# Attention and expert gathers of a transformer layer in one program block, with the expert queries computed between the rows, and weights in batches of four

## The reference

```python
def peer_block(hb, w_q, sub_keys, u_tab, v_tab):
    q = (hb @ w_q).reshape(n, PEER_HEADS, PEER_QDIM)             # 8 heads, 2 x 128
    s1 = jnp.einsum('nhd,kd->nhk', q1, sub_keys[0])              # 128 scores a half
    s2 = jnp.einsum('nhd,kd->nhk', q2, sub_keys[1])
    v1, i1 = lax.top_k(s1, 16); v2, i2 = lax.top_k(s2, 16)
    top_s, pos = lax.top_k(v1[..., :, None] + v2[..., None, :], 16)
    g = jax.nn.softmax(top_s)
    act = jax.nn.gelu(jnp.einsum('nhkd,nd->nhk', u_tab[expert], hb))
    return jnp.einsum('nhk,nhkd->nd', g * act, v_tab[expert])
```

## Time and profile before

| what | us |
|---|---|
| median of 3 runs | 3617.58 (3615.84 to 3617.71) |
| profiled execution, its own time | 3618.12 |
| its span, first to last instruction | 3616.3 |
| busy: PE, DVE, POOL, ACT | 2665.0, 2239.5, 1350.0, 430.3 |
| first gather of the latents' experts, of the last layer's | 1964.35, 2936.63 |

### The profile page before, as it was taken

One profiled execution on the slowest core, in us unless ns is written; L12 is line 12 of the kernel. 1 busy time (PEld: TensorE's weight loads), 2 busy tenths in 40 slices (PEclk: granted clock), 3 DMA queues, 4 the chain that ended last, 5 costly groups with the idle time before them and its releaser, 6 DMA issues. The chain is left out here.

```text
span 3616.3 us, 24758 instructions
## 1 busy us (share of the span) xinstructions
PE 2665.0 (74%) x7868; PEld 1434.3 (40%) x7868; DVE 2239.5 (62%) x5144; ACT 430.3 (12%) x1222; POOL 1350.0 (37%) x1082
## 2 busy tenths in 40 slices
PE   6788839459958648993575877878866757787777
PEld 1423324437625446741344333333333533333333
DVE  1316655686666686665867777777526157777774
ACT  0200001110000110000110111111112101111111
POOL 0000002365564265664444444545300034545442
PEclk9999869569988759996887898888878878888898
DMA  7154426389988378998776999999850259999996
GB/s 256 70 204 152 152 97 239 119 286 335 389 301 315 119 259 305 392 358 314 238 246 241 421 420 420 420 420 420 348 184 24 88 207 421 421 421 421 421 422 248
DMA packets 258261, 1043.06 MB, mean 288 GB/s; under 512 B 20342, under 2 KB 36838, under 8 KB 192340
## 3 DMA queue, kind: packets, MB, share of 16 engines
q0 software_dynamic: 147456, 805.37, 56.5%
q1 hardware_dynamic: 102928, 220.69, 16.8%
q10 hardware_dynamic: 7748, 15.43, 1.2%
HBM read 1038.69 MB, written 2.72 MB: 288 GB/s over the span
## 5 line engine op out<-in xcount | busy, mean ns | idle before, releaser
L1077 POOL DMA_INDIRECT sb_beside_slots<-in_peer_uv,sb_beside_chosen x512 | 610.8, 1193 | 706.1 <-issue 363.3
L1001 PE MATMUL psum<-sb_last_rows,sb_last_H 128*128 128x512 f32 x768 | 401.4, 687 | 168.7 <-ACT sb_last_H L985 168.7
L1001 PE MATMUL psum<-sb_latents_rows,sb_latents_diag 128*128 128x512 f32 x640 | 351.2, 714 | 165.0 <-ACT sb_latents_diag L985 165.0
L1050 DVE SCALAR_TENSOR_TENSOR sb_beside_slots<-sb_beside_slots,sb_beside_H 128x1024 f32<-128x1024 f32 x256 | 312.3, 1221 | 228.8 <-DMA sb_beside_slots<-in_peer_uv,sb_beside_chosen 227.2
L894 POOL DMA_INDIRECT sb_last_rows<-in_peer_uv,sb_last_scores x192 | 236.7, 1233 | 363.0 <-PE psum L1001 257.2
L1069 DVE SCALAR_TENSOR_TENSOR sb_xc<-sb_beside_slots,sb_beside_small,sb_xc 128x1024 f32<-128x1024 f32 x254 | 325.5, 1282 | 8.0 <-DMA sb_beside_slots<-in_peer_uv,sb_beside_chosen 6.2
L1001 PEld LDWEIGHTS psum<-sb_last_rows,sb_last_H 128*128 128x128 f32 x768 | 166.8, 222 | 402.7 <-issue 203.7
L894 POOL DMA_INDIRECT sb_latents_rows<-in_peer_uv,sb_latents_scores x160 | 203.2, 1270 | 292.8 <-PE psum L1001 247.3
L921 DVE SCALAR_TENSOR_TENSOR sb_last_rows<-sb_last_rows,sb_last_H 128x1024 f32<-128x1024 f32 x192 | 231.3, 1222 | 110.3 <-DMA sb_last_rows<-in_peer_uv,sb_last_scores 110.3
L172 PE MATMUL psum<-sb_f_arena,sb_f_ring 128*128 128x256 f32 (+1 forms) x1344 | 292.9, 381 | 5.4 <-issue 5.4
L1001 PEld LDWEIGHTS psum<-sb_latents_rows,sb_latents_diag 128*128 128x128 f32 x640 | 144.5, 231 | 370.6 <-ACT sb_latents_diag L985 194.2
(11 more groups left out here) (468 smaller groups left out, 3733.9 us busy)
## 6 DMA issues: line engine op xcount, KB each, us to landing
sb_f_ring<-in_w_ff SPq DMA_DIRECT2D x32, 2048.0 KB, 12.8
sb_context_ring<-in_ada_w SPq DMA_DIRECT2D x24, 2048.0 KB, 7.9
sb_f_ring<-in_w_in SPq DMA_DIRECT2D x8, 2048.0 KB, 14.4
sb_f_ring<-in_w_in SPq DMA_DIRECT2D x6, 1904.0 KB, 12.6
sb_context_ring<-in_peer_w_q SPq DMA_DIRECT2D x8, 1024.0 KB, 10.0
sb_beside_slots<-in_peer_uv,sb_beside_chosen POOLq DMA_INDIRECT x512, 6.2
sb_f_ring<-in_w_out SPq DMA_DIRECT2D x4, 2048.0 KB, 7.8
sb_latents_ring<-in_peer_w_q SPq DMA_DIRECT2D x4, 2048.0 KB, 10.8
```

The lines of the kernel that those rows point to most:

```text
L1001: done = e.matmul(st.pair(("acc", g))[:, half, :], diag[:, n % (2 * ROWS), :], v_of(n)[:, half * 512:(half + 1) * 512], start=(f == 0 and ...
L1050: e.scalar_tensor_tensor(out=self.u_slot[s % 4], in0=self.u_slot[s % 4], scalar=1.0, in1=self.H[:, s // (PH * TOPK), :], op0=ALU.mult, op1 ...
L1077: return e.indirect_dma_start(out=to, out_offset=None, in_=self.table, in_offset=bass.IndirectOffsetOnAxis(ap=at, axis=0), element_offset= ...
```

## The change

1. For the latents' and the last layer, `attention` no longer runs a block of its own. It returns its engine programs as a `Front`, and `experts` runs them at the head of its own block. The context's block stays.
2. The 16 query blocks move from the end of `attention` into `experts`. Blocks 0 to 3 stand before the rows; block t + 4 is computed in turn t, its queries ahead of the turn's sums on PE and its scores after half of them. w_q comes in eight loads of 1 MB (256 columns) into the halves of ring slot 2. `SC` holds three heads, not all.
3. The turns are ordered head by head, both tiles of a head in turn, so both accumulators stay open.
4. `weights` takes 4 rows, not 8, and the diagonals have four batches of room. Routing of the turn after next is spread over the four batches.
5. The head loop runs `more(2)`. What is left of `Beside` runs right after the second norm.
6. `layer_memory` lays all buffers out once; slots for rows overlay attention's buffers. There are 14 of them in the latents' layer and 15 in the last.

```diff
-    st.run(sync, scalar, vector, gpsimd, tensor, beside and beside.sems[0])
+    if context:
+        st.run(sync, scalar, vector, gpsimd, tensor)
+    return Front(st, sync, scalar, vector, gpsimd, tensor, lambda e: e.wait_ge(*st.computed(("qkv", 2, h_tiles[-2]))))
...
         for i in range(n_heads + 2):
-            more(1)
+            more(2)
...
+        more(Beside.STEPS)
+        if not context:
+            return
...
+    turns = [(g, f) for f in range(PH) for g in range(NT)]
...
+    wq_half = [sb["ring"][2][:, 2048 * j:2048 * (j + 1)].rearrange("p (k n) -> p k n", k=KT) for j in range(2)]
+    bank_q, bank_sc = [psum[:, 4 + j, 0:S] for j in range(2)], [psum[:, 6 + j, 0:S] for j in range(2)]
...
+    ahead = lambda t: t + 4 if t + 4 < 2 * PH else None
+
+    def sync(e):
+        front.sync(e)
+        front.slot_free(e)
+        for f in range(PH):
+            if f >= 2:
+                e.wait_ge(q_done, 2 * f - 2)
+            e.dma_start(wq_half[f % 2], wq[:, :, f * S:(f + 1) * S]).then_inc(wq_in[f % 2], 16)
+        e.nop()
...
+        keep_scores(0)
+        keep_scores(1)
         for q in (0, 1):
             half_of(q, 0)
             half_of(q, 1)
             route_sums(e, own, rt, top_ready)
             picks(q)
+            keep_scores(2 + q)
         for q in range(len(turns)):
             more = q + 2 < len(turns)
...
+            for j in range(TOPK // BATCH):
+                b = TOPK // BATCH * q + j
+                for r in range(BATCH):
+                    dot(b * BATCH + r)
+                if more and j < 2:
+                    half_of(q + 2, j)
+                if more and j == 2:
+                    route_sums(e, own, rt, top_ready)
+                if more and j == 3:
+                    picks(q + 2)
                 weights(b)
...
+            if ahead(q):
+                keep_scores(ahead(q))
...
+            if b >= 4:
+                e.wait_ge(added, BATCH * (b - 3))
+            for r in range(BATCH):
+                e.activation(diag[:, (b % 4) * BATCH + r, :], C("ident"), ACT.Copy, scale=w[:, r:r + 1]).then_inc(diag_ready, 1)
...
+        queries(0)
+        queries(1)
+        scores(0)
+        queries(2)
+        scores(1)
+        queries(3)
+        scores(2)
+        scores(3)
+        for q in range(len(turns)):
+            if ahead(q):
+                queries(ahead(q))
+            sums(4 * q)
+            sums(4 * q + 1)
+            if ahead(q):
+                scores(ahead(q))
+            sums(4 * q + 2)
+            sums(4 * q + 3)
...
+    slots = [ring[:, j // 2, 2048 * (j % 2):2048 * (j % 2 + 1)] for j in range(4)] + [work[:, 0:2048], work[:, 2048:4096]]
+    slots += [pair(gains, 0), aux[:, 0:2048], pair(mod, 0), *spare]
```

More of the change, by code:

```diff
@@ L271, in attention @@
         plan += wq_plan[7:8]
[L272 to L275, removed]
+    wq_of = lambda b: ("q", b // 2 * 2 + 1)
+    wq_cols = lambda b: (b % 2) * P
     wqkv_of = {g[1]: g for _, g, _ in plan if g[0] == "qkv"}
@@ L987, in scalar @@
+        keep_queries(0)
+        keep_queries(1)
+        keep_queries(2)
         route(0)
+        keep_queries(3)
         route(1)
         for q in range(len(turns)):
-            weights(2 * q)
+            weights(4 * q)
+            if ahead(q):
+                keep_queries(ahead(q))
+            weights(4 * q + 1)
+            weights(4 * q + 2)
             if q + 2 < len(turns):
                 route(q + 2)
-            weights(2 * q + 1)
+            weights(4 * q + 3)
     def tensor(e):
-        for n in range(n_rows):
-            g, f = turns[n // TOPK]
-            k = n % TOPK
-            e.wait_ge(diag_ready, n + 1)
-            for half in range(2):
-                done = e.matmul(st.pair(("acc", g))[:, half, :], diag[:, n % (2 * ROWS), :], v_of(n)[:, half * 512:(half + 1) * 512],
-                                start=(f == 0 and k == 0), stop=(f == PH - 1 and k == TOPK - 1))
-            done.then_inc(added, 1)
@@ L1005, in experts, with queries, scores @@
-    st.run(idle, scalar, vector, gpsimd, tensor)
+        front.tensor(e)
+        def queries(b):
+            f = b // 2
+            e.wait_ge(wq_in[f % 2], 16 * (f // 2 + 1))
+            if b >= 2:
+                e.wait_ge(q_copied, b - 1)
+            matmuls(e, bank_q[b % 2], [(wq_half[f % 2][:, k, (b % 2) * P:(b % 2 + 1) * P], hT[:, k, :]) for k in range(KT)]).then_inc(q_done, 1)
+        def scores(b):
+            e.wait_ge(q_copied, b + 1)
+            if b >= 2:
+                e.wait_ge(sc_copied, b - 1)
+            for j in range(2):
+                done = e.matmul(bank_sc[b % 2][:, j * P:(j + 1) * P], qbuf[b % 2][:, j * P:(j + 1) * P], sub[:, 2 + b % 2, :], start=True, stop=True)
+            done.then_inc(sc_done, 1)
@@ new lines, in sums @@
+        def sums(b):
+            for n in range(b * BATCH, (b + 1) * BATCH):
+                g, f = turns[n // TOPK]
+                k = n % TOPK
+                e.wait_ge(diag_ready, n + 1)
+                for half in range(2):
+                    done = e.matmul(st.pair(("acc", g))[:, half, :], diag[:, n % (4 * BATCH), :], v_of(n)[:, half * 512:(half + 1) * 512],
+                                    start=(f == 0 and k == 0), stop=(f == PH - 1 and k == TOPK - 1))
+                done.then_inc(added, 1)
@@ L1818, in expert_memory @@
[L1818 to L1829 removed]
+    sb["ring"] = [ring[:, j, :] for j in range(3)]
@@ L1830, in expert_memory @@
+    sb["slots"] = slots
     return sb
@@ L1868, in build @@
         st.run(load, idle, idle, idle, idle)
-        def layer(layer, part, held, beside=None):
-            with ExitStack() as inner:
-                attention(nc, sems, psum, attention_memory(mem(inner, f"{part}_"), held, part), A, C, xs, kept, layer, part, beside)
         with ExitStack() as both:
```

202 lines of the change are left out of this document (100 added, 102 removed).

## The result

The kernel after takes 3563.02 us (median of four runs, 3561.24 to 3564.98) against 3617.57 (3615.84 to 3617.71) before: a ratio of 0.985, 95% interval 0.983 to 0.987. That is 54.5 us less, with 3564 predicted. The same kernel run again among the experiments gave 0.9847 (0.9818 to 0.9877).

The account below looks back on a forecast made before the run. The prediction took both expert stages as bound by the gathers' DMA rate. Last layer -46.8 and latents' layer -6.6 gave -53.4 us on 3618.1: 3564.7, and 3564 against the median; range 3548 to 3592.

Parts of the forecast that it names:

- The gathers bound both stages: Both expert stages run at the gathers' DMA rate, 2.50 us a row, 639 us a layer.
- First gather 23.7 us after the first query: Ahead of the expert stages: last layer +23.7 for +75.7, -52.0 us; latents' layer +23.8 for 83.6, -59.8 us.
- Four loads a stage at 3.05 us: Inside each expert stage: four 1 MB w_q loads remain, 3.05 us each, adding 12.2 us a layer.
- End -7: End of each expert stage: batches of four leave 16 matmuls, not 32; 10 to 13.5 us instead of 19.0, -7.
- Head loop +48: Latents' head loop: two Beside steps an iteration, 3.5 us a step, lengthen it by 48 us; bounds +38 to +62.
- Rival 1: Latents' head loop: steps run at VectorE's pace, 3.14 us each; 10 us less, 3554; chance 0.17.
- Rival 3: Head loop and stages: steps 4.0 us (+14), more w_q loads (+12), no gain at one end (+7); 3575 to 3597; chance 0.22.
- Rival 4: Both expert stages: PE becomes the bound through slow-starting bursts, up to +340 us a layer; time near 3640; chance 0.07.
- Rival 5: Latents' expert stage: 14 slots leave DMA gaps; 3591 at 2.60 us a row, 3617 at 2.70; chance 0.05.
- Behind the heads everything keeps its length: Latents' layer behind the head loop: output projection, norm and h2T keep their length, 0 us change.

Follow-up runs that it names:

- the control: The changed kernel run once more, unchanged, among the experiments, compared with the kernel before: ratio 0.9847 (0.9818 to 0.9877).

## Why the prediction came out

- *The gathers bound both stages; the gain lies ahead of the first and behind the last.* Shown: DMA share 1.01 and 1.00, leaving the loads out brings 24.1 us, and batches of eight touch the end alone.
- *First gather 23.7 us after the first query.* 23.2 and 21.8, and 24.1 and 24.7 in the control. The working is right, and so is its size. That the last layer gained 1.9 us more than forecast is chance of one execution: its first 32 query matmuls ran at full clock (7.14 us, before 8.77), in the control at 0.58 (10.0 us), and there the gain is 51.0, 1.0 less than forecast.
- *Four loads a stage at 3.05 us.* 3.0 by the run without them. The Trainium skill's figure for a 1 MB load by itself ("DMA: Bandwidth & Descriptors", Measured), 6.15 us, would have made it 24.6 a stage, an estimate; these runs show half of that behind queued gathers. The page measured loads that GpSimd issues, here SyncE issues them. The last layer's 13.9 holds 2.0 that the run without loads still has; where they come from stays open.
- *End -7.* -8.6 and -8.2: sixteen matmuls took 7.1 us after a pause of 1.3 in the latents' layer and 8.8 after one of 2.8 in the last, both inside my 7.0 to 10.1, of which I had taken a middle value. Which layer gets the shorter end changes from run to run; in two runs it is 13.4.
- *Head loop +48, because steps are held by gathers at 3.5 us.* +51.8. The split was nearly right. It had 6.3 us an iteration on VectorE alone and 7.0 with the waits for gathers. Measured, the 13 full intervals from scaling to scaling take 94.6 us, 7.3 each; 10.7 of the 12.4 us of waits fall inside them, 0.8 each, which leaves 6.45. So the term was some 0.3 us an iteration too small, 0.1 in the waits and 0.15 in the rest, and over 13 iterations that is 3.6 of the 3.8 us missing. One long wait, 3.4 us, is in it: in the control the 13 intervals take 93.1 us, of which waits are 0.7 each, as forecast. From the copy to the last scaling the control has 213.6 us, +51.2. That the waits come from three steps on one round of POOL's order is half shown: with rounds of four, 7.2 of the 12.4 us (10.0 in the control) remain (6.4 before dots, 0.8 before accumulations), and what holds those is open.
- *Rival 1* (VectorE's pace) is refuted by the 12.4 us. *Rival 3* had one of its parts only, the dearer steps, at 3.8 us and not 14.
- *Rival 4* (PE as the bound). PE is busy 33 us a turn of 40, and the granted clock of the stages went up, 0.86 to 0.91, where the rival needed it to stay at the 1.2 GHz level. By the Trainium skill's rule ("TensorE: Matmul & The Clock Gate", HAM oscillation) a burst that follows a long enough wait starts at half clock. The trace agrees in single bursts, such as the last layer's end above, where four matmuls after a pause of 2.8 us took 3.31 us and the last four 1.88. Over a stage the loss did not grow, and the bursts of half the size came with shorter pauses. Between 20 us behind the latents' first gather and the last dot PE has 31 pauses over 0.5 us before, 4.1 us in the median and 161 us in all, and 41 after, 2.8 and 108 us. With batches of eight in the new structure there are 26, 4.9 and 139 us, and the clock is 0.90; so longer bursts alone don't bring back the 0.86, and what set the stage's clock is not shown.
- *Rival 5* (gaps from fewer slots). Ten would do, eight would not.
- *Behind the heads everything keeps its length* was wrong by -3.0 and -2.6 us, from the load that moved. The 2.6 are part of the -4.2 ahead of the last layer's first query; its other 1.6 is less than that stretch moves without the change (227.0 us in the kernel before, 224.4 in the same kernel with the new order of the gathers). The misses have both signs, +3.8, +3.3 and +1.7 against -3.0, -4.2, -2.8, -2.5 and small ones, and sum to -3.5 us; to that extent the forecast's closeness, 1 us from the median, is luck.

## What to carry to other kernels

When a queue of transfers bounds a stage, ask what must be done before its first transfer and after its last; put the rest of the preparation into the stage, and check each engine there against the pace of a turn. Fill-in work on VectorE costs its full time inside a loop that VectorE nearly fills, and little where VectorE waits for another engine (here 4.4 us for four steps): count the waits by place before choosing where it goes, and leave alone a wait for a small load, which more gathers only lengthen. And look at the order in a queue that carries two streams: one of them waiting for a younger event than the other holds both, here for 33 us of the whole kernel.

## What the hardware showed that was not expected

- The same 260 PE instructions of the head loop were busy 43.6 us at a granted clock of 0.91 when the loop took 63.9 us, and 63.9 us at 0.65 when it took 116.4. Here it cost next to nothing: VectorE sets the loop's pace and waited for PE 2.2 us in it. No run here has a loop whose pace PE sets.
- In the expert stages the clock rose from 0.86 to 0.91 as PE's busy time rose from 498 to 528 us of 642, and was 0.89 to 0.94 in the variants of the kernel after.
- The same 32 query matmuls at the head of the last layer's routing took 7.1 us in four executions and 10.0 to 10.2 in seven, and moved the first gather by 3 us.
- The 512 KB rows for the late modulation landed in 4.9 us (median) with three gathers about, in 8.5 beside 1 MB loads of w_q and in 8.7 beside gathers.
- With ten row slots the gathers kept 412 GB/s, with eight 361.
